# Expert matrices in chunks of 1024 columns, activation rounding on ScalarE for small jobs, one row tile a chunk in native fp32

## The reference

```python
def swiglu(h, w1, w3, w2):
    return (jax.nn.silu(h @ w1) * (h @ w3)) @ w2

def moe_swiglu(h, router, w1, w3, w2):
    logits = (h @ router).astype(F32)
    top_v, top_i = lax.top_k(logits, TOP_K)
    gates = jax.nn.softmax(top_v, axis=-1)
    dense_gate = jnp.sum(jax.nn.one_hot(top_i, N_EXPERTS, dtype=F32) * gates[..., None], axis=-2)
    y = jnp.zeros(h.shape, F32)
    for e in range(N_EXPERTS):
        y = y + swiglu(h, w1[e], w3[e], w2[e]).astype(F32) * dense_gate[..., e:e + 1]
    return y.astype(h.dtype)
...
    return rmsnorm(h, final_norm)
```

## Time and profile before

| | us |
|---|---|
| median of 3 runs | 1572.08 (1569.6 to 1574.46) |
| the profiled execution | 1573.55 |
| its span, first to last instruction | 1571.5 |
| PE busy | 1457.9 (93%) |
| DVE busy | 1131.2 (72%) |
| ACT busy | 912.0 (58%) |

### The profile page before, as it was taken

The page is one execution under the profiler, slowest core; times in us unless marked ns, Lnnn a source line. Parts: engine busy times, 40 slices in busy tenths (PEclk is TensorE's granted clock), DMA queues, the critical chain, the costliest instruction groups (busy, mean ns, idle before and its releaser), DMA issues.

```text
span 1571.5 us, 19090 instructions
## 1 busy us (share of the span) xinstructions
PE 1457.9 (93%) x7242; PEld 1148.2 (73%) x7242; DVE 1131.2 (72%) x1214; ACT 912.0 (58%) x891; POOL 51.8 (3%) x64
## 2 busy tenths in 40 slices
PE   5999979999899997899999999999899899899897
PEld 4776669999777665788788776767677677677675
DVE  1615245555351525888888899999999999999997
ACT  2222244444222222767677688788787887887885
POOL 0130000000023000000000000000000000000000
PEclk9999979999999997999999999999999999999998
DMA  8532613551742064699799999999999999999991
GB/s 300 176 107 80 211 57 124 199 180 62 243 136 101 27 225 177 216 370 368 276 362 362 330 380 396 392 393 396 393 396 393 395 393 395 394 394 394 394 397 46
DMA packets 190708, 433.45 MB, mean 276 GB/s; under 512 B 5678, under 2 KB 30276, under 8 KB 190660
## 3 DMA queue, kind: packets, MB, share of 16 engines
q1 hardware_dynamic: 190468, 432.25, 74.8%
q0 software_dynamic: 192, 0.53, 0.1%
HBM read 431.71 MB, written 1.05 MB: 275 GB/s over the span
## 4 chain that ended last, share of the span: by engine, by line
PE 64%; DVE 18%; issue 11%; ACT 5%; DMA 1%; SPq 0%; DVEq 0%; ACTq 0%; PEldq 0%
PE bank L1715 25%; PE bank L1311 12%; DVE ring_lo L1240 11%; PE bank L1288 7%; PE bank L1293 5%; PE bank L1569 4%; ACT w_hi L764 3%; PE bank L1727 3%; PE bank L1659 2%; PE bank L1278 2%; PE bank L1609 1%; DVE h L1098 1%; PE bank L1464 1%; DVE y_lo L1087 1%; ACT r L661 0%
## 5 line engine op out<-in xcount | busy, mean ns | idle before, releaser
L1240 DVE TENSOR_TENSOR ring_lo<-ring,w_hi 128x2048 fp32r<-128x2048 f32 (+1 forms) x352 | 753.7, 2188 | 46.6 <-ACT w_hi L764 46.0
L764 ACT ACTIVATE w_hi<-ring 128x2048 fp32r<-128x2048 f32 (+1 forms) x352 | 627.3, 1833 | 30.9 <-PE bank L1715 30.8
L1715 PE MATMUL bank<-w_hi,xg 128*128 128x512 f32 x1120 | 413.2, 397 | 8.7 <-DVE ring_lo L1240 8.7
L1715 PE MATMUL bank<-ring_lo,xg 128*128 128x512 f32 x896 | 367.1, 410 | 26.4 <-DVE ring_lo L1240 23.2
L1715 PEld LDWEIGHTS bank<-w_hi,xg 128*128 128x128 f32 x1120 | 212.7, 190 | 53.7 <-DVE ring_lo L1240 10.4
L1715 PEld LDWEIGHTS bank<-ring_lo,xg 128*128 128x128 f32 x896 | 169.1, 189 | 101.0 <-DVE ring_lo L1240 68.8
L1715 PE MATMUL bank<-ring_lo,at_hi 128*128 128x512 f32 x448 | 184.0, 411 | 20.7 <-DVE at_hi L1211 16.1
L1715 PE MATMUL bank<-w_hi,at_hi 128*128 128x512 f32 x448 | 176.5, 394 | 0.0
L1715 PEld LDWEIGHTS bank<-ring_lo,at_hi 128*128 128x128 f32 x448 | 84.0, 187 | 67.5 <-issue 31.4
L1038 DVE TENSOR_TENSOR wf_lo<-ring,wf_hi 128x1024 fp32r<-128x1024 f32 x66 | 80.5, 1223 | 62.2 <-ACT wf_hi L677 62.2
L677 ACT ACTIVATE wf_hi<-ring 128x1024 fp32r<-128x1024 f32 x66 | 69.6, 1058 | 72.6 <-PE bank L1311 71.1
(11 more groups left out here) (319 smaller groups left out, 1476.2 us busy)
## 6 DMA issues: line engine op xcount, KB each, us to landing
ring<-in_moe_w SPq DMA_DIRECT2D x168, 2048.0 KB, 13.0
ring<-in_ffn_w SPq DMA_DIRECT2D x18, 1536.0 KB, 6.7
ring<-in_w_in SPq DMA_DIRECT2D x6, 2048.0 KB, 15.1
ring<-in_w_out SPq DMA_DIRECT2D x8, 1024.0 KB, 4.9
ring<-in_ffn_w SPq DMA_DIRECT2D x3, 2048.0 KB, 7.6
ring<-in_w_in SPq DMA_DIRECT2D x4, 1024.0 KB, 16.1
ring<-in_xa_wkv SPq DMA_DIRECT2D x2, 2048.0 KB, 12.8
ring<-in_w_in SPq DMA_DIRECT2D x2, 1184.0 KB, 5.6
```

The costliest lines, as they stand in the source:

```text
L764: act.activation(w_hi[:, i % NB, 0:cols.stop - cols.start], ring[:, slot_of(u), cols], ACT.Copy)\
L1240: dve.tensor_tensor(ring_lo[slot_of(u)][:, cols], ring[:, slot_of(u), cols], w_hi[:, i % NB, 0:cols.stop - cols.start], sub).then_inc(S["l ...
L1715: ins = mm(dst, st_, mv, start=opens, stop=closes, skip_group_check=small)
```

## The change

**Chunks.** w1 and w3 come in three chunks of 1024 columns and one of 512 (`CHUNKS`). A unit of w1 or w3 holds 512 rows by 1024 columns (in the last chunk 1024 by 512), so a row in memory has 4096 bytes and not 2048. Two units make the chunk. A chunk's products take two banks each for w1 and w3, the same four in each chunk. w2 stays in units of 512 rows. The order is w1 of chunk d, then the turn of chunk d-1, w3 of chunk d, w2 of chunk d-1. At the job's end the last turn stands between the two w2 units of the chunk before.

**Activations.** All steps of a chunk are done for both halves in a row: two copies, 16 turn matmuls, two Silus, two products, two roundings. In small jobs the rounding of the activations (`at_hi`) is ACT's, with its own place one piece after Silu. The distances to the last piece of a unit are 4 for w1's rows and for Silu, 3 for w3's rows; in full jobs 4, 4, and 5.

**Native row tile.** In small jobs one of four row tiles of the first w2 unit of each chunk (columns 2048 to 3072 of the unit) is neither rounded nor subtracted. PE multiplies it by the unrounded activations in fp32, two matmuls with 64 stationary columns in place of four. The piece of ACT and DVE is 1024 columns wide there, four times a job.

**Other.** `final_norm` is loaded after the last job into slot 1 of the ring, and not ahead of the first. Some buffers move.

```diff
-JOB_UNITS = [(1, 0), (3, 0)] + [x for c in range(1, NCH) for x in ((1, c), (3, c), (2, c - 1))] + [(2, NCH - 1)]
+CHUNKS = (2, 2, 2, 1)
...
+    units = of(1, 0) + of(3, 0)
+    for d in range(1, NCH):
+        units += of(1, d) + of(3, d) + of(2, d - 1)
+    return units + of(2, NCH - 1)
...
+WHOLE = tuple((2, d, 0) for d in range(NCH))
...
-def after(unit):
-
-    return LAST[UNIT_OF[unit]] + LEAD
...
+def rows1_at(d, small):
+
+    return last_piece(1, d) + (4 if small else NB)
+
+
+def rows3_at(d, small):
+
+    return min(last_piece(3, d) + (3 if small else NB), JOB_PIECES - 4)
+
+
+def turned_at(d, small):
+
+    return JOB_PIECES - 2 if d == NCH - 1 else last_piece(1, d + 1) + (4 if small else NB + 1)
...
     u, lo, hi = CUTS[i]
-    return u, slice(lo, hi)
+    return u, slice(3072 if small and JOB_UNITS[u] in WHOLE and lo == 2048 else lo, hi)
...
                     else:
-                        dst, src = v3(slot, 0, 4096, KT), A[f"moe_w{w}"][0, ex, :, FC * c:FC * c + FC]
+                        rows = 4096 // width * P
+                        dst = v3(slot, 0, 4096, 4096 // width)
+                        src = A[f"moe_w{w}"][0, ex, rows * part:rows * part + rows, CHUNK0[d]:CHUNK0[d] + width]
...
+                def turned_hi(d):
+                    act.wait_ge(S["j_m" if small else "j_tps"], cn[d])
+                    for x in halves(d):
+                        if small:
+                            i = act.activation(at_hi[:, 4 * x:4 * x + 4, 0:SMALL], s_act[x], ACT.Copy)
...
+                    for d in range(NCH):
+                        if small and i == turned_at(d, True):
+                            small_silu(d)
+                        if i == turned_at(d, small) + small:
+                            turned_hi(d)
+                    for d in range(NCH):
+                        if i == rows1_at(d, small):
+                            rows1(d)
+                        if small and i == rows3_at(d, True):
+                            small_rows3(d)
...
-                    dve.tensor_copy(at_hi[:, :, 0:SMALL], s_act).then_inc(S["j_th"], 1)
-                    dve.wait_ge(S["j_th"], cn[c])
...
+                        if small and (w, d, part) in WHOLE and cols.start == 0:
+                            for half in range(2):
+                                at = 2 * 2 * FC + FC * half
+                                mm(ps[6 + half][0:SMALL, :], s_act[0][:, 2, :], ring[:, slot_of(u), at:at + FC],
+                                   start=False, stop=False, skip_group_check=True)
...
+                for d in range(1, NCH):
+                    pe.wait_ge(S["j_s"], cn[d - 1])
+                    rows_of(1, d)
...
+                    turn(d - 1)
+                    rows_of(3, d)
+                    pe.wait_ge(S["j_t"], cn[d - 1])
...
+                    products(2, d - 1, 0)
+                    if d == NCH - 1:
+                        turn(d)
+                    products(2, d - 1, 1)
```

More of the change, by code:

```diff
@@ L35 @@
 FC = 512
-NCH = FE // FC
+CHUNKS = (2, 2, 2, 1)
+NCH = len(CHUNKS)
+CHUNK0 = tuple(FC * sum(CHUNKS[:d]) for d in range(NCH))
 MAX_JOBS = N_EXP + 3
@@ L150, in build @@
                    for i in range(RING)]
+        cst_at = (nc.sbuf_base + 31) // 32 * 32
         cst = sb("cst", [P, CONST_W])
@@ L716, in yrow_out, with halves @@
                 act.activation(y_hi[:, half, :], ps[6 + half][:, :], ACT.Copy).then_inc(S["j_ya"], 1)
-            def transposed(n):
-                act.wait_ge(S["j_tps"], n)
-                act.activation(at_hi[:, :, :], v3(ps[4], 0, 512, 4), ACT.Copy).then_inc(S["j_th"], 1)
+            def halves(d):
+                return range(CHUNKS[d])
             gather_hi(1)
@@ L746, in job @@
                             yrow_out(j, half)
-                    for c in range(NCH):
-                        last = i == JOB_PIECES - 1 if c == NCH - 1 else i == after((1, c + 1)) + 1
-                        if not small and i == after((1, c)):
-                            first_rows(c)
-                        if last and small:
-                            small_silu(c)
-                        elif last:
-                            transposed(cn[c])
-                        if small and i == after((1, c)) + 1:
-                            first_rows(c)
-                        if small and i == after((3, c)):
-                            act.wait_ge(S["j_h3"], cn[c])
-                            act.activation(s_rows[1], ps[2 * (c % 2) + 1][:, :], ACT.Copy).then_inc(S["j_a"], 1)
-                    u, cols = job_cols(i)
+                    for d in range(NCH):
[8 more added lines that the diff above has]
+                            small_rows3(d)
+                    u, cols = job_cols(i, small)
                     if cols.start == 0:
@@ L1216, in job @@
                             yrow_out(j, half)
[L1217 to L1227 removed]
+                    for d in range(NCH):
+                        if not small and i == rows3_at(d, False):
+                            rows3(d)
+                        if small and i == turned_at(d, True):
+                            small_hidden(d)
+                        if i == turned_at(d, small) + small:
+                            turned_lo(d)
                     for t in range(TT):
[L1229 removed]
+                        if i == rows3_at(0, small) + t:
                             combined(j, t)
[L1231 removed]
+                    if i == rows3_at(0, small) + TT:
                         dve.wait_ge(S["j_cv"], j * 2 + 2)
@@ L1694, in products @@
                         pe.wait_ge(S["lo_ready"], pieces + (i + 1))
-                        n = (cols.stop - cols.start) // FC
                         steps = []
-                        for part in range(n):
+                        for at in range(cols.start, cols.stop, FC):
                             if w == 2:
-                                f, half = (cols.start // FC + part) // 2, part % 2
-                                dst, opens, closes = ps[6 + half], c == 0 and f == 0, c == NCH - 1 and f == 3
+                                half, f = at // FC % 2, 4 * part + at // (2 * FC)
+                                dst, opens, closes = ps[6 + half], d == 0 and f == 0, d == NCH - 1 and f == 3
@@ L1714, in products @@
                         for x, (dst, st_, mv, opens, closes) in enumerate(steps):
-                            ins = mm(dst, st_, mv, start=opens, stop=closes, skip_group_check=small)
+                            ins = mm(dst[:, :], st_, mv, start=opens, stop=closes, skip_group_check=small)
                             if x == 0:
@@ new lines, in products, with rows_of, turn @@
+                    return ins
+                def rows_of(w, d):
+                    for part in range(CHUNKS[d]):
+                        ins = products(w, d, part)
+                    ins.then_inc(S[f"j_h{w}"], 1)
+                def turn(d):
+                    pe.wait_ge(S["j_a"], cn[d])
+                    for x in range(CHUNKS[d]):
+                        for f in range(4):
+                            rows = slice(FC * x + P * f, FC * x + P * f + P)
+                            if small:
+                                for w3 in range(2):
+                                    c0 = 256 * w3 + SMALL * f
+                                    i = mm(ps[4 + x][:, c0:c0 + SMALL], s_rows[w3][:, rows], fold, start=True, stop=True)
+                            else:
+                                i = pe.transpose(ps[4 + x][:, P * f:P * f + P], j_act[:, rows], ident)
```

174 lines of the change are left out of this document (92 added, 82 removed).

## The result

The changed kernel takes 1581.89 us (median of 18 runs, 1575.58 to 1587.35), the kernel before 1572.46 (18 runs, 1567.58 to 1575.83). The ratio is 1.0062, with a 95% interval of [1.0046, 1.0079]: slower by 0.6%. The forecast was +5.4 us, measured are +9.4. The profiled execution has a span of 1583.2 us, 11.7 more than before.

A forecast was written before the change was run, and what follows sets the result against it. DVE was taken to pace the small jobs, PE the full ones. Full jobs -4.9, small jobs with the end +10.3, sum +5.4 us: median 1572.08 becomes 1577.5, slower by 0.34%, range 1562 to 1593.

The forecast's parts named there:

- DVE's relief: Small jobs: 6.6 us a job less work on DVE, yet its waits for ACT grow, jobs 112 to 113 us.
- the tail: After the last small job, PE ends 0.66 us later, the native pair being half hidden.
- the full jobs: The 2.02 us hole at the first chunk goes in both, with 1.6 of slow clock in the second: -4.9 us.
- First and second wait: In each 1024-column chunk of small jobs DVE waits for ACT: 1.87 us after the turn, 1.15 at w3's row copy.
- The walk: Small job followed row by row through pieces and waits: 112.1 us, 113.0 in five of six; 1573 to 1584, chance 0.5.
- The halved piece: Cut to 1024 columns in small jobs (4.3 us off DVE), it only lengthens DVE's wait at ACT's copy of w3's rows.
- The native pair: In small jobs' first w2 units on PE, a native fp32 matmul takes 0.865 us, the pair 1.73, the unit 4.61.
- The stall at the job's start: ACT may round piece 2 only when PE begins the old job's last piece; DVE stands 0.85 us in five jobs.
- Rival 3: Dearer native matmuls or a falling PE clock after more holes: 1584 to 1600 us, chance 0.13.
- The wait for the last whole chunk's activations: Full jobs: PE waits 0.4 us for these activations in each of the two, since they are taken at piece 40.
- Loads: Wider w1 and w3 rows take a small job's loads from 111.9 to 108.7 us; nobody waits, so costed at nothing.
- Rival 1: DVE's relief comes through, loads bind small jobs at 108.7 us: total 1542, or 1557 if load rate stays; chance 0.12.

The follow-up runs named there:

- the best version: Changed kernel with the turn split, no native row tile in the last w2 unit, w1's row copy one piece later in the third chunk only: 1557.05 us, ratio 0.9906.

## Why the prediction was right or wrong

**DVE's relief is swallowed by waits:** right, and shown both ways. Busy time fell to 100.23 (forecast near 100), the waits for ACT rose from 1.5 to 10.1 (forecast 13). Giving ACT's rounding back to DVE changed no job by more than 0.05 us, and without native tiles the middle stretches are the same to 0.01. The forecast total owes something to luck: the small jobs cost 6.1 us more than worked out and the tail 0.7, and the full jobs gave back 1.0 of it. The terms below say where.

**First and second wait:** 1.87 and 1.15 forecast, 1.93 and 1.12 in the second double chunk; the first one has 0.75 and 1.12. There DVE begins its product 7.63 us after PE's start on the last w1 piece (1142.50 to 1150.13) and not 6.47, since it has the combining of the old job and work for the next one ahead of it, and so it waits less. The walk used one chunk's rows for both. The double chunk between two Silus of ACT is 29.92 us (1148.16 to 1178.08) for 29.8, the stretch after it 25.51 for 25.4. The walk's reason held in part: moving the copy took the wait down by its 0.98, but the stretch by 0.55 only, and splitting the turn brought more than any move of a copy. The walk was right as a sum over that loop; it does not tell what taking one term out would bring, since the next wait stands close behind.

**The halved piece "only makes this wait longer":** right for the first two chunks, wrong for the third. There PE's hole ahead of the activations is 0.45 us with it and 2.38 without, which is worth 0.8 to 2.4 us a job. The prediction did not ask what ACT and DVE have ahead of the third chunk's activations.

**The native pair:** 0.865 a matmul was forecast, 0.93 measured, and the unit 4.92 for 4.61. The term was mis-sized by 0.3: 0.13 in the pair, 0.10 in the four matmuls behind it, 0.08 in the eight ahead of it. The rows from which it came have natives only, with 128 stationary columns; here each pair has 64 and stands between split matmuls. Which of the two makes it dearer is not shown. From the third turn's 0 (PE's start on the last w1 piece ahead of it) to the next job's first piece it was 26.86 us (1197.92 to 1224.78) for 26.4: 0.31 is this unit, and 0.15 its later start (9.82 for 9.67).

**The stall at the job's start:** the place and the jobs (five of six) were right, its price 0.85 was too small. PE begins the last piece 3.87 us after the gather (1221.84 to 1225.71), not 3.59: the native pair's mis-sizing once more. DVE waits 1.06, and the job pays 1.15, in two of the five jobs 1.34 and 1.53, where a low clock follows PE's hole of 1.81 us. This is 2.0 of the 6.1 us by which the small jobs' +15.75 exceeds +9.6. The remaining 4.1 are 0.7 a job in six: 0.46 at the job's end as said, 0.11 in each of the two stretches from turn to turn, and 0.03 ahead of the first turn.

**Rival 3, the falling clock,** was given little because holes of 1.0 us cost nothing before. It came true in small measure, 0.6 us in all, at a hole nearly twice as long. The kernel before has a longer one than the prediction read, once in each small job, and its clock is 1.00 too:

```profile
1137.41 0.50 PE L1715 MATMUL bank<-ring_lo,at_hi 128*128 128x512 f32 x1 [1.56 <-DVE at_hi L1211]
```

In the small jobs of these traces the clock falls only near a hole of 1.8 us or more, and not near each of them. The Trainium skill, "TensorE: Matmul & The Clock Gate", A second HAM failure mode, has micro-idles between groups make the clock swing. These traces don't bear that out for holes of up to 1.56 us: in the best version's job, with several of up to 1.0 us, the clock is 1.00.

**Full jobs:** -5.9 for -4.9. The cause is shown by the edit that moves Silu alone and takes 2.3 and 3.75 us off. The wait for the last whole chunk's activations, forecast at 0.4 in each, is there with 0.29 in PE's timeline of the second job:

```profile
865.77 0.49 PE L1778 MATMUL bank<-w_hi,at_hi 128*128 128x512 f32 x1 [0.29 <-DVE at_lo L1280]
```

Hole and wait together give the first job's -2.0 (2.3 less 0.3). In the second the forecast was 2.02 + 1.6 - 0.4 = 3.2 and 3.9 came. The hole was priced by its idle time; from start to start (770.30 to 772.71 in the trace of before) it is 2.41 for a matmul of 0.23, so 2.2. Which rows hold the other 0.5 stays open.

**Loads:** no engine waited for one in the jobs of any kernel, so costing them at nothing was right. Rival 1's bound of 108.7 was not reached: the shortest job is 110.0, with 401 GB/s. Whether it holds, and whether rows of 4 KB load faster than rows of 2 KB, stays open. No run has the wide rows, or w2's moved unit at the job's end, undone by itself.

**The tail:** +1.4 for +0.66. In the run with the copy later and without the last native pair it is 14.95, as before, so all of it is that pair: it is not half hidden.

## What to carry to other kernels

Taking work off the busiest engine was worth nothing here where it then waited for another. Ask for the loop that closes there (here PE's turn, ACT's Silu, copy and piece, DVE's three buffered pieces) and make the longest uninterrupted step in it shorter. A step that is doubled in size is better placed in halves between the pieces, as the split turn was; more buffers between the engines might do the same, which no run tried. Measure such changes by job periods or by stretches between fixed rows, which repeat to 0.03 us, and price a gain only up to the next wait in the same loop.

## What was not expected of the hardware

A hole of 1.8 to 2.4 us on PE goes with a granted clock of half for 3 to 4 us in some jobs and not in others of the same execution, with the same rows around it: four of six times at the hole of 2.38 us, three of five times at the 1.81 us hole of the changed kernel (the second, third and fifth). The price of the job's first stretch was 1.15, 1.15, 1.53, 1.15 and 1.34 there, so one of the three lower clocks cost nothing.

The stages ahead of the experts, which no edit here touches, differ by up to 10 us between executions. Windows of the same stretch in the kernel before and in the one with the native tile added to it:

```profile
200.00:300.00 100.00, 93.37 (x591) 83.02 (x592) 52.64 (x72) 43.09 (x53) 0.00 (x0) 0.92 0.32 111
```

```profile
200.00:300.00 100.00, 92.39 (x631) 84.53 (x630) 56.39 (x76) 45.48 (x56) 0.00 (x0) 0.98 0.38 135
```

The granted clock is 0.92 in one and 0.98 in the other, and more instructions fit into the second. The totals go with it: of 15 runs of the kernel before, the shortest (1564.70) has a mean clock of 0.983 and the longest (1575.70) one of 0.973. So a total of one run can't tell 4 us.
